# Sample rows of one output projection in fp32 on four column groups in the first sweep, their scores in three parts, the last rows in halves

## Chip, cores and metric

The kernel runs on one core of one Trainium2 chip. The metric is the device time of one execution in microseconds (us); lower is better. PE is TensorE, ACT ScalarE, DVE VectorE, POOL GpSimd and SP the engine that issues the DMAs.

## What is computed

Two layers of a streaming encoder, for 1024 prompt rows and for 32 sample rows of running streams (width 1024). The even layer ends with an output projection over the two branch outputs, the odd layer is causal attention with a forget bias:

```python
# even layer
o = jnp.einsum('ble,ed->bld', jnp.concatenate([ya, yb], axis=-1), w_out)   # 2048 x 1024 weights
x = x + rmsnorm(o, g_post)
# odd layer, for each of 8 heads
s = q @ k_all.T * scale + f_q - f_k          # prompt rows: 1024 keys; sample rows: 256 cached + 32 own
s = where(key_pos <= query_pos, s, -inf)
y = silu(z) * (softmax(s) @ v_all)
x = x + rmsnorm(y @ w_out_odd, g_post)
```

## The kernel before

**Precision.** Nearly all products are made from two parts. A value is split into a high part in fp32r and the rest in fp32r (`WH`/`WL` for weights, `HH`/`HL` and `YSH`/`YSL` for activations), and each product is three fp32r matmuls: high by high, low by high, high by low. Attention's scores, its probabilities times values, and the products with the state of the recurrence are true fp32 matmuls; the trace shows each of these as two records.

**Even output projection (`out_step`, L1034 on).** The weights have 16 blocks of 128 rows by 1024 columns. The 1024 prompt rows are eight tiles of 128 (t = 0 to 7), the 32 sample rows are tile 8 (`SMP`, also `NB`). Each tile has a pair of PSUM banks (`PAIRS`: t = 0, 4, 8 have banks 6 and 7; 1, 5 have 0 and 1; 2, 6 have 2 and 3; 3, 7 have 4 and 5). The work is done in three sweeps over all 16 weight blocks: tiles 0 to 2, tiles 3 to 5, tiles 6, 7 and `SMP`. A step of one weight block in one sweep is a unit (u = 0 to 47), and each sweep loads its 16 blocks again. In a unit a prompt tile takes six matmuls of 512 columns. The sample tile takes four: its high rows and its low rows stand side by side in the stationary operand, so two products per bank do. Units 46 and 47 come together: tile `SMP` first, then 6, then 7, each over both units.

**How a unit's weights get there.** `load_rows` on SP loads 512 KB to one of two raw buffers, `WRAW[:, idx % 2]`. It waits until the low parts of the unit two earlier are made (`w_low`, `oe_lo`), since these read the same raw buffer. ACT (`prepare`) splits off the high part of the activations (`token_high`) and of the weights (`split_rows`), POOL and DVE (`lows`) each make the low part of one half of the weights' columns. `WHS`/`WLS` and `YSH`/`YSL` have three slots; `prepare(u)` waits until unit u - 3 is done (`p_chunk`, three counts for a unit). PE waits in `units_ready(u)`. At u = 5 SP also issues four other loads of 512 KB. In the sweeps 1 and 2 the tiles of the sweep before are normalised between the units: ACT `squares`, DVE `gained`, `mean`, `residual`, `normed_x1`, PE `turn_h1` (transposes, before units k = 6, 7 and 13 of the sweep), ACT `h1_high`, DVE `h1_low`; SP stores rows at k = 6 and 15 and loads others at k = 11 and 12. Each engine works strictly in the order that is written out.

**Scores (`scores`, L1163 on).** In a turn of the loop over heads PE runs the scores, transposes and values of head t between the projections of head t + 1. The sample rows' scores are one fp32 matmul of 288 columns on 32 stationary columns, to partitions 0 to 31 of `PB[3]`. In the first seven heads DVE adds the mask of the last 32 keys and the forget bias and takes maxima; in the last head (`masked`) a bf16 matmul of the identity with `MASKD` adds the mask in PSUM.

**End.** The odd output projection ends with tile 7 in two halves of 512 columns. After each half ACT squares it, DVE multiplies it by the gain (`out_gained`), then `out_mean`, ACT's root and `out_rows` (one DVE instruction of 1024 columns), and SP stores 512 KB.

## Time and profile before

| | us |
|---|---|
| median of 3 runs | 1559.44 (1559.19 to 1560.11) |
| the profiled execution | 1558.85 |
| its span, first to last instruction | 1557.1 |
| PE busy, granted clock | 1526.9 (98%), 0.998 |
| first sweep of the even output projection | 65.3 |
| second sweep | 68.6 |
| third sweep, to the start of the last matmul of tile 7 | 61.6 |

The profiled execution's time is 1.75 us above its span. Start times count from the first instruction. A matmul's duration in a record is longer than its distance from the next one, since matmuls overlap in the array; distances between starts are what counts. An engine's "idle before" names who released it.

### The profile page before, as it was taken

The numbers are of one execution on the slowest core, as the hardware profiler recorded it, in microseconds if no ns is written. First come the engines' busy times: TensorE is split into PE (matmuls) and PEld (weight loads), VectorE is DVE, ScalarE is ACT, GpSimd is POOL, SyncE is SP. The second block draws the span as 40 slices with busy tenths as digits, with TensorE's granted clock in tenths as the row PEclk, the third lists the DMA queues.
The fourth block names the chain that finished last, engine by engine and source line by source line (L and its number), as shares of the span: only waits on it lengthen the run. The fifth ranks groups of instructions, "written<-read, shape, count | busy, mean of one in ns | idle before, by whom it ended". The sixth has DMA issues, their size and how long they took to land.

```text
span 1557.1 us, 26394 instructions
## 1 busy us (share of the span) xinstructions
PE 1526.9 (98%) x9409; PEld 1413.2 (91%) x9409; DVE 830.2 (53%) x1921; ACT 675.4 (43%) x1258; POOL 444.6 (29%) x268
## 2 busy tenths in 40 slices
PE   7999999999999999999999899999999999999998
PEld 6999999999999999988888898999999999988786
DVE  5547777776884231446475244545454554545532
ACT  6434443443233322345465344544454545455321
POOL 1214544452121111244343231322222222314200
PEclk9999999999999999999999999999999999999999
DMA  5122122213102111254456446624241424213122
GB/s 156 43 71 75 61 86 79 73 33 98 42 27 58 41 40 40 69 185 152 162 187 144 62 76 46 76 47 70 36 75 42 68 43 72 47 59 143 55 99 72
DMA packets 129513, 121.11 MB, mean 78 GB/s; under 512 B 10291, under 2 KB 113293, under 8 KB 129453
## 3 DMA queue, kind: packets, MB, share of 16 engines
q1 hardware_dynamic: 129452, 120.32, 31.7%
q8 instruction: 37, 0.61, 0.2%
q14 instruction: 24, 0.19, 0.0%
HBM read 101.64 MB, written 18.66 MB: 77 GB/s over the span
## 4 chain that ended last, share of the span: by engine, by line
PE 90%; ACT 4%; DVE 3%; issue 2%; DMA 0%; POOL 0%; SPq 0%; ACTq 0%; DVEq 0%; POOLq 0%
PE PB L767 85%; PE PB L771 5%; ACT L1358 1%; ACT L1826 1%; DVE SB L1955 0%; ACT SB L1920 0%; ACT WH L1352 0%; DVE XT L1958 0%; DVE M L1958 0%; ACT SQJ L1392 0%; DMA XS<-in_x_prompt_dram 0%; DMA WOR<-in_w_out_odd_dram 0%; DVE XS L1955 0%; DVE ST L1958 0%; POOL WL L633 0%
## 5 line engine op out<-in xcount | busy, mean ns | idle before, releaser
L767 PE MATMUL PB<-HH,WH 128*128 128x352 f32 x1872 | 626.5, 335 | 2.6 <-DVE HL L1951 1.6
L767 PE MATMUL PB<-HH,WL 128*128 128x352 f32 x1872 | 602.3, 322 | 0.0
L767 PE MATMUL PB<-HL,WH 128*128 128x352 f32 x1872 | 601.4, 321 | 0.0
L767 PEld LDWEIGHTS PB<-HH,WH 128*128 128x128 f32 x1872 | 351.9, 188 | 17.2 <-issue 9.2
L767 PEld LDWEIGHTS PB<-HL,WH 128*128 128x128 f32 x1872 | 352.9, 189 | 5.8 <-issue 3.3
L767 PEld LDWEIGHTS PB<-HH,WL 128*128 128x128 f32 x1872 | 352.1, 188 | 0.0
L633 POOL TENSOR_TENSOR WL<-WRAW,WH 128x1024 fp32r<-128x1024 f32 x81 | 199.3, 2460 | 525.6 <-ACT WH L1352 518.8
L1352 ACT ACTIVATE WH<-WRAW 128x1024 fp32r<-128x1024 f32 x112 | 118.0, 1053 | 14.4 <-DMA WRAW<-in_w_out_even_dram 6.3
L1920 ACT ACTIVATE SB<-SB,small 128x128 f32<-128x128 f32 (+8 forms) x72 | 53.9, 748 | 105.9 <-DVE small L1955 105.9
L767 PE MATMUL PB<-PT,VTOK 128*128 128x128 f32 (+2 forms) x624 | 81.5, 274 | 0.0
L767 PEld LDWEIGHTS PB<-PT,VTOK 128*128 128x128 f32 (+1 forms) x624 | 78.3, 191 | 1.5
L767 PE MATMUL PB<-KALL,QT 128*128 128x512 f32 (+4 forms) x208 | 78.0, 482 | 0.0
L1951 DVE TENSOR_TENSOR Y<-PB,Y 128x128 f32 (+3 forms) x72 | 20.2, 280 | 108.3 <-PE PB L767 108.2
L661 POOL TENSOR_TENSOR M<-M,CBT 128x512 f32<-128x512 f32 (+1 forms) x48 | 62.2, 1322 | 47.4 <-ACT M L1544 47.4
L767 PE MATMUL PB<-WH,YSH 128*128 128x512 f32 x192 | 75.1, 391 | 0.0
L767 PE MATMUL PB<-WL,YSH 128*128 128x512 f32 x192 | 74.8, 389 | 0.0
L685 POOL TENSOR_TENSOR WL<-WRAW,WH 128x512 fp32r<-128x512 f32 x30 | 53.5, 1785 | 65.5 <-ACT WH L1352 65.5
L1352 ACT ACTIVATE PT<-PB 128x512 f32<-128x512 f32 (+3 forms) x112 | 45.9, 447 | 55.4 <-PE PB L771 55.3
L1951 DVE TENSOR_TENSOR UG<-UG,ZG 128x1056 f32<-128x1056 f32 x8 | 12.2, 1529 | 105.5 <-ACT ZG L1372 105.5
L767 PE MATMUL PB<-WH,YSL 128*128 128x512 f32 x172 | 66.9, 389 | 0.0
L711 POOL TENSOR_TENSOR NRM<-QT 128x352 f32<-128x352 f32 x24 | 20.0, 833 | 145.8 <-ACT QT L1352 145.8
L1951 DVE TENSOR_TENSOR SB<-PB,MASKD 128x128 f32<-128x128 f32 (+1 forms) x63 | 17.6, 279 | 82.4 <-PE PB L767 82.4
(316 smaller groups left out, 2424.7 us busy)
## 6 DMA issues: line engine op xcount, KB each, us to landing
WRAW<-in_w_out_even_dram SPq DMA_DIRECT2D x48, 512.0 KB, 3.5
WRAW<-in_w_in_even_dram SPq DMA_DIRECT2D x44, 512.0 KB, 3.8
WRAW<-in_w_in_odd_dram SPq DMA_DIRECT2D x32, 512.0 KB, 8.2
ACSB<-acs_rows SPq DMA_DIRECT2D x16, 528.0 KB, 5.3
NFB<-nf_rows SPq DMA_DIRECT2D x8, 656.0 KB, 3.8
XS<-in_x_prompt_dram SPq DMA_DIRECT2D x8, 512.0 KB, 6.3
XT<-in_x_prompt_dram SPq DMA_DIRECT2D x8, 512.0 KB, 5.2
x_rows<-OG SPq DMA_DIRECT2D x8, 512.0 KB, 5.8
```

The costliest lines, as they stand in the source:

```text
L633: pool.tensor_tensor(WL[:, slot(w), :, :], WRAW[:, slot(w), :, :], WH[:, slot(w), :, :].bitcast(f32), ALU.subtract).then_inc(S("w_low"), 1)
L661: pool.tensor_tensor(m, m, CBT[0:rows, g, b0:b0 + nb, 0:rows], ALU.mult).then_inc(S("m"), 1)
L685: pool.tensor_tensor(WLS[SLOT3[u % 3]][:, HALF:D], raw[:, HALF:D], WHS[SLOT3[u % 3]][:, HALF:D].bitcast(f32), ALU.subtract).then_inc(S("w_ ...
L711: last = pool.tensor_tensor(NRM[:, n, cols], src, src, ALU.mult)
L767: return pe.matmul(out, lhsT, rhs, start=start, stop=stop)
L771: return pe.transpose(out, in_, IDENT[0:n, 0:n])
L1352: return act.activation(out, in_, ACT.Copy, scale=scale)
L1358: act.add_instruction(mybir.InstLoadActFuncSet(name=nc.get_next_instruction_name(), act_func_set_id=LN_EXP_SET, ins=[], outs=[]))
L1826: act.activation(Y1[:, p, :], Y1[:, p, :], ACT.Silu).then_inc(S("zs"), 1)
L1920: act.activation(SB[0:rows, 0:width], SB[0:rows, 0:width], ACT.Exp, scale=SCALE, bias=NBIAS[0:rows, :], accum_out=RSUM[0:rows, :]).then_in ...
L1951: return dve.tensor_tensor(out, a, b, op)
```

## The change

It has three parts. First, the sample rows leave the third sweep. In each unit of the first sweep PE makes four fp32 matmuls of 256 columns, which use the activations and the raw weights without splitting (`out_sample`); each writes to its own 32 partitions of `PB[4]`. They stand ahead of the unit's tiles, in unit 0 behind them. The load of a raw buffer now waits for them too (units 2 to 17). After unit 15's, ACT copies the sums to `SMPS` ahead of the squares, and tile 3 waits for the copy, as `PB[4]` is its bank. Second, in seven heads the sample rows' scores are three fp32 matmuls of 96 columns on three groups of partitions of `PB[3]`, followed by the mask as a bf16 matmul, and DVE takes three parts without a mask. Third, at the end `out_mean(8)` goes ahead of the last `out_gained`, and the last rows are made and stored in two halves.

```diff
+            if idx >= W_OE + 2 and idx < W_OE + 18:
+                sp.wait_ge(S("smp_mm"), idx - 1 - W_OE)
...
-            sp.wait_ge(S("y_done"), n + 1)
-            sp.dma_start(dst, X1T[n % 2][0:rows, :]).then_inc(S(f"y_stored{n % 2}"), 16)
+            parts = 2 if n == len(FINAL) - 1 else 1
+            for c in range(parts):
+                cols = slice(c * (D // parts), (c + 1) * (D // parts))
+                sp.wait_ge(S("y_done"), n + 1 + c)
+                sp.dma_start(dst[:, cols], X1T[n % 2][0:rows, cols]).then_inc(S(f"y_stored{n % 2}"), 16)
...
-                if t != SMP:
-                    mm(out, ysl[:, own], wh[:, cols], start=False, stop=False)
+                mm(out, ysl[:, own], wh[:, cols], start=False, stop=False)
...
+        def out_sample(u):
+
+            k = u % 16
+            pe.wait_ge(S(f"w_raw{u % 2}"), loads_of_slot(tile_no(W_OE + u, 1, 0)))
+            y = YB[:, k, SEQ:TOK] if k < 8 else YA[:, k - 8, SEQ:TOK]
+            raw = WRAW[:, (W_OE + u) % 2, :, :].rearrange("p k c -> p (k c)")
+            for q in range(4):
+                last = mm(sample_part(q), y, raw[:, q * PART:(q + 1) * PART], start=k == 0, stop=k == 15)
+            last.then_inc(S("smp_mm"), 1)
...
-            tiles = range(3 * sweep, 3 * sweep + 3)
+            tiles = range(3 * sweep, min(3 * sweep + 3, NB))
...
+                if 0 < u < 16:
+                    out_sample(u)
...
+                        if t == 3:
+                            pe.wait_ge(S("smp_out"), 1)
...
-                    out_step(t, u, j).then_inc(S("p_chunk"), 1)
+                    out_step(t, u, j).then_inc(S("p_chunk"), 2 if t == NB - 1 else 1)
+                if u == 0:
+                    out_sample(u)
...
-        for j, t in ((2, SMP), (0, 6), (1, 7)):
+        for j, t in ((0, 6), (1, 7)):
             out_step(t, 46, j)
-            out_step(t, 47, j).then_inc(S("p_chunk"), 2)
+            out_step(t, 47, j).then_inc(S("p_chunk"), 3)
...
+            if b == NB and not masked:
+                for k in range(3):
+                    cols = slice(SEQ + k * PART3, SEQ + (k + 1) * PART3)
+                    mm(sample_scores(k), q, KALL[:, cols], stop=k < 2)
+                mm(sample_scores(2)[:, PART3 - DEC:PART3], IDENTB[0:rows, 0:rows], MASKD[0:rows, 0:rows],
+                   start=False).then_inc(S("sc_mm"), 1)
+                return
...
-            return copy(high[:, 0:2 * P + DEC], src[:, 6 * P:TOK])
+            return copy(high[:, 0:2 * P], src[:, 6 * P:SEQ])
...
-                    copy(OGT[2][0:DEC, c * HALF:(c + 1) * HALF], bank[DEC:2 * DEC, :]).then_inc(S("o_sq"), 1)
+                    act.wait_ge(S("p_chunk"), 3 * (W_OE + 46))
+                    copy(OGT[2][0:DEC, c * PART:(c + 1) * PART], SMPS[c * DEC:(c + 1) * DEC, :]).then_inc(S("o_sq"), 1)
                 else:
...
+            if u == 15:
+                act.wait_ge(S("smp_mm"), 16)
+                copy(SMPS[:, :], PB[4][:, 0:PART]).then_inc(S("smp_out"), 1)
...
             else:
-                tt(YSL[u % 3][:, 0:2 * P], src[:, 6 * P:SEQ], high[:, 0:2 * P].bitcast(f32), ALU.subtract)
-                last = tt(high[:, 2 * P + DEC:2 * P + 2 * DEC], src[:, SEQ:TOK], high[:, 2 * P:2 * P + DEC].bitcast(f32),
-                          ALU.subtract)
+                last = tt(YSL[u % 3][:, 0:2 * P], src[:, 6 * P:SEQ], high[:, 0:2 * P].bitcast(f32), ALU.subtract)
...
-                dve.wait_ge(S("o_sq"), 2 * place(t) + c + 1)
+                dve.wait_ge(S("o_sq"), 2 * place(t) + (2 if t == SMP else c + 1))
...
-                    tt(og[0:DEC, cols], bank[0:DEC, :], og[0:DEC, cols], ALU.add).then_inc(S("o_g"), 1)
+                    q = 2 + c
+                    dve.tensor_copy(og[0:DEC, q * PART:(q + 1) * PART], SMPS[q * DEC:(q + 1) * DEC, :]).then_inc(S("o_g"), 1)
...
-                    own = width if not project else width - rows
-                    n = (own + 511) // 512
+                    parts = project and i == NB
+                    own = width - rows if project and not parts else width
+                    step = PART3 if parts else 512
+                    n = (own + step - 1) // step
...
-                    if project:
+                    if own == width:
+                        order(dve.memset(MX[0:rows, n:n + 1], -3.0e38))
+                    else:
...
-                        c0, c1 = k * 512, min(own, k * 512 + 512)
-                        order(dve.tensor_tensor_reduce(SB[0:rows, c0:c1], PB[3 + k][0:rows, 0:c1 - c0],
-                                                       NFB[0:rows, key0 + c0:key0 + c1], 1.0, -3.0e38,
+                        c0, c1 = k * step, min(own, (k + 1) * step)
+                        part = slice(k * DEC, (k + 1) * DEC) if parts else slice(0, rows)
+                        scored = sample_scores(k) if parts else PB[3 + k][0:rows, 0:c1 - c0]
+                        order(dve.tensor_tensor_reduce(SB[0:rows, c0:c1], scored,
+                                                       NFB[part, key0 + c0:key0 + c1], 1.0, -3.0e38,
                                                        ALU.add, ALU.max, MX[0:rows, k:k + 1]))
...
-        def out_rows(n):
+        def out_rows(n, parts=1):
...
-            stt(X1T[n % 2][0:rows, :], FOG[n % 2][0:rows, :], ORR[0:rows, n:n + 1], X1T[n % 2][0:rows, :],
-                ALU.mult, ALU.add).then_inc(S("y_done"), 1)
+            for c in range(parts):
+                cols = slice(c * (D // parts), (c + 1) * (D // parts))
+                stt(X1T[n % 2][0:rows, cols], FOG[n % 2][0:rows, cols], ORR[0:rows, n:n + 1], X1T[n % 2][0:rows, cols],
+                    ALU.mult, ALU.add).then_inc(S("y_done"), 1)
...
-        for h in range(6, 18):
+        for h in range(6, 17):
             out_gained(h)
             if h % 2 == 1:
                 out_mean(h // 2)
                 out_rows(h // 2)
+        out_mean(8)
+        out_gained(17)
+        out_rows(8, parts=2)
```

## Rows read from the trace of the kernel before

**Rows 1.** Page, first part: busy time, share of the span, instructions.
```profile
PE 1526.9 (98%) x9409; PEld 1413.2 (91%) x9409; DVE 830.2 (53%) x1921; ACT 675.4 (43%) x1258; POOL 444.6 (29%) x268
```

**Rows 2.** Busy time by stretch: engines with instructions, PEclk, DMA share, GB/s.
```profile
649.97:715.30 65.33, 65.33 (x290) 54.06 (x290) 31.01 (x40) 26.89 (x40) 30.21 (x17) 1.00 0.48 161
```

**Rows 3.** The chain that ended last, in order of time: start us, us, what.
```profile
745.75 20.46 PE PB L767 x90
...
811.25 18.19 PE PB L767 x80
...
831.51 2.33 DVE XT L1958
```

**Rows 4.** Timeline of PE: start us, us, operation, count [idle before, releaser].
```profile
133.51 1.06 PE L767 MATMUL PB<-CT,ST 128*128 128x128 f32 x8
134.50 1.09 PE L767 MATMUL PB<-M,XD 128*64 128x128 f32 x16
135.52 0.43 PE L767 MATMUL PB<-HH,WH 128*128 128x352 f32 x1
```

**Rows 5.** The same timeline, asked for the stretch 134.45 to 134.52 only.
```profile
134.50 0.33 PE L767 MATMUL PB<-M,XD 128*64 128x128 f32 x2
```

**Rows 6.** Timeline of PE: scores of the sample rows in one head.
```profile
970.90 1.04 PE L771 MATMUL PB<-IDENT,SB 128*128 128x128 f32 x8
971.87 0.67 PE L767 MATMUL PB<-KALL,QT 128*32 128x288 f32 x2
972.47 0.43 PE L767 MATMUL PB<-HH,WH 128*128 128x352 f32 x1
972.73 0.32 PE L767 MATMUL PB<-HL,WH 128*128 128x352 f32 x1
```

**Rows 7.** Timeline of PE: scores of the sample rows in the last head.
```profile
1483.36 0.67 PE L767 MATMUL PB<-KALL,QT 128*32 128x288 f32 x2
1483.96 0.18 PE L767 MATMUL PB<-MASKD,IDENTB 32*32 32x32 bf16 x1
1484.07 0.50 PE L767 MATMUL PB<-WH,YH 128*128 128x512 f32 x1
```

**Rows 8.** Timelines of SP, ACT and POOL: one load and its two splits.
```profile
673.00 2.49 SPq L483 DMA_DIRECT2D WRAW<-in_w_out_even_dram  x2
...
676.42 1.06 ACT L1352 ACTIVATE WHC<-WRAW 128x1024 fp32r<-128x1024 f32 x1 [1.24 <-DMA WRAW<-in_w_out_even_dram]
...
677.56 1.80 POOL L685 TENSOR_TENSOR WLC<-WRAW,WHC 128x512 fp32r<-128x512 f32 x1 [3.02 <-ACT WHC L1352]
...
679.38 0.33 SPq L483 DMA_DIRECT2D WRAW<-in_w_out_even_dram  x1
```

**Rows 9.** Timelines of SP and ACT: the load after four others.
```profile
664.46 0.33 SPq L483 DMA_DIRECT2D WRAW<-in_w_out_even_dram  x1
...
670.03 1.06 ACT L1352 ACTIVATE WH<-WRAW 128x1024 fp32r<-128x1024 f32 x1 [3.01 <-DMA WRAW<-in_w_out_even_dram]
```

**Rows 10.** Timelines of ACT and DVE at the end of the first sweep.
```profile
712.76 0.58 ACT L1665 ACTIVATE JUNK<-PB 128x512 f32<-128x512 f32 x1
...
713.53 1.40 DVE L1951 TENSOR_TENSOR OG<-PB,POSTB 128x512 f32<-128x512 f32 x2
```

**Rows 11.** Timelines of POOL, SP, ACT and PE in the third sweep.
```profile
781.52 1.80 POOL L685 TENSOR_TENSOR WL<-WRAW,WH 128x512 fp32r<-128x512 f32 x1 [2.28 <-ACT WH L1352]
...
798.31 0.33 SPq L483 DMA_DIRECT2D WRAW<-in_w_out_even_dram  x1
...
803.10 1.06 ACT L1352 ACTIVATE WH<-WRAW 128x1024 fp32r<-128x1024 f32 x1 [0.39 <-DMA WRAW<-in_w_out_even_dram]
...
833.88 1.09 PE L771 MATMUL PB<-IDENT,XT 128*128 128x128 f32 x8 [0.83 <-DVE XT L1958]
```

**Rows 12.** Timelines of DVE at the end of the kernel, and DMA.
```profile
1551.36 0.69 DVE L1951 TENSOR_TENSOR FOG<-PB,POSTF 128x512 f32<-128x512 f32 x1 [4.87 <-ACT JUNKF L1787]
...
1552.68 1.28 DVE L1958 SCALAR_TENSOR_TENSOR X1T<-FOG,small,X1T 128x1024 f32<-128x1024 f32 x1 [0.50 <-ACT small L1603]
...
out_dram<-X1T SPq DMA_DIRECT2D x1, 512.0 KB, 2.6
```

**Rows 13.** Timeline of DVE after the third sweep.
```profile
855.79 1.28 DVE L1958 SCALAR_TENSOR_TENSOR OG<-OG,small,XT 128x1024 f32<-128x1024 f32 x1 [1.11 <-DMA XT<-in_x_prompt_dram]
```

## What I expect and why

> **What bounds the kernel.** I read the page's busy times first: PE is at work for 98% of the span [rows 1]. That alone doesn't say that PE is the bound in each stage, so next came the busy times by stretch: in the first sweep of the even output projection PE is busy for all of its 65.33 us, ACT and POOL for less than half of it [rows 2]. The chain of waits in order of time says the same of the later sweeps: long pieces of nothing but matmuls, 90 in 20.46 us and 80 in 18.19 us, so 0.2273 us for one of 512 columns, with a short break for a DVE result once in a while [rows 3]. There the reader is to see two things: a matmul removed is worth 0.2273 us as long as PE stays the bound, and a unit takes PE 18 x 0.2273 = 4.09 us in the first two sweeps and 16 x 0.2273 = 3.64 us in the third. Whether PE stays the bound depends on the feeding of the weights, which I read in the timelines of SP, ACT and POOL [rows 8].
>
> **Matmuls removed.** Tile SMP had 4 matmuls in each of 16 units: 64 x 0.2273 = -14.5 us, all of it PE time in the third sweep. A unit there takes PE 12 x 0.2273 = 2.73 us.
>
> **The sample step added.** Each of 16 units of the first sweep gets four fp32 matmuls of 256 columns with 32 stationary columns. Their price rests on whether the four run side by side. The trace has a case with two column groups: 16 records of 64 stationary columns take 1.02 us, from 134.50 to 135.52, while 8 records of 128 stationary columns over as many moving columns take 0.99 [rows 4]. So two halves cost what one whole costs. The narrow look shows the first two started within 0.02 us [rows 5]. I take four groups to do what two do. One fp32 matmul of 288 columns on 32 stationary ones, in the same mode, takes 0.60 us to the next matmul's start [rows 6]; 256 columns take at most a ninth less, so 0.55. There is more at both ends. The records on 128 stationary columns follow each other by about 0.11 us; 8 of them from 133.51 would end at 134.41, and the next kind starts at 134.50: 0.09 to go in [rows 4]. And the first matmul afterwards is followed only after 0.26 us (972.47 to 972.73) where 352 columns otherwise take 0.16: 0.10 to come out [rows 6]. In all 0.55 + 0.09 + 0.10 = 0.74, with some 0.02 for three more starts 0.76 us. 16 x 0.76 = +12.2 us. The bounds: 0.55 if the ends are hidden (8.8 us), and 4 x 0.5 + 0.2 if nothing overlaps (35 us). I take 0.76, since rows 4 and 6 show both ends paid.
>
> The Trainium skill gives 2.38 times for three column tiles (TensorE: Matmul & The Clock Gate, Measured speedup vs the span model), thus less than three; an estimate from that would put some 0.1 us more on each step, and 2 us on the sum.
>
> **Waits in the first sweep.** A raw buffer is now free only when PE has read it. A load takes 3.42 us until ACT splits it (673.00 to 676.42), ACT's split is 1.14 us ahead of POOL's, POOL's takes 1.80, and SP reacts at 679.38: 6.38 us for one turn of a buffer [rows 8]. Before, it could begin as soon as the low part was made; now it begins about 0.65 us into unit u - 2, where PE's sample step ends. For most units that is hidden: two units are 2 x 4.85 = 9.7 us, and 0.65 + 6.4 = 7.0. It isn't hidden in unit 2, since unit 0's sample step stands at its end: 4.8 + 6.35 = 11.1 us against 9.7, a wait of 1.4. Unit 6 has its load behind four others, where a load took 5.57 us (664.46 to 670.03) [rows 9]: 2.2 us more, which eats the slack of 2.7 nearly up; I add 0.3 for queueing. Together +1.7 us, between 0 and 4.
>
> **The border of the first two sweeps.** On ACT `prepare(17)` stands ahead of the copy to `SMPS` and of four squares. Its load now starts 0.65 us into unit 15 and its split ends at 0.65 + 3.4 + 1.1 = 5.15, the copy at 5.5; unit 16 would start at 4.85, and its first tile waits for the copy: 0.7. The squares, then DVE's products by the gain (0.77 behind, 712.76 to 713.53, 1.40 for two [rows 10]), hold the banks of tiles 4 and 5: the second tile could start at 5.5 + 1.6 + 0.8 = 7.9 but is due at 6.9. I count 0.9 for tiles 4 and 5. Together +1.6 us, between 0 and 3. Queued behind the copy on ACT are the squares and `prepare(18)`, which has a unit to spare.
>
> **The third sweep stops being bound by PE.** Here is the main step. Two units now take PE 5.46 us, but a raw buffer's turn is 6.38, and there are two buffers: a unit per 3.19 us at best. The low part of unit 33 is made at 781.52 + 1.80 = 783.32 [rows 11], 0.6 us ahead of unit 32 (783.9). 14 turns later, unit 47's is ready at -0.6 + 14 x 3.19 = 44.1 us after the sweep's start; units 46 and 47 then take 24 x 0.2273 = 5.5. That makes 49.6 against 61.8 before: a gain of 12.2, not 14.5. Five transfers of rows share the queue in this sweep; with two of them a load took 4.79 us until its split (798.31 to 803.10), 1.4 more [rows 11]. Some 2.2 us of that fall on the last turns, which have no slack. Last, PE transposes tile 5 ahead of unit 45 and before waited 0.83 us for DVE there [rows 11]; DVE makes its 2.33 us instruction [rows 3] only behind its low part of unit 46. That part is made at about 42 us, so the transposes come at 44.2, unit 45 at 45.1 and the end at 45.1 + 2.7 + 5.5 = 53.3 us. The gain is 8.5; waits +6.1, between 2.3 and 9. I carried these waits through all 48 units; done the same way for the kernel before, with its own waits, this gives 0.3 us less than recorded.
>
> **Behind the sweep.** The rows that tile 7 is added to are loaded late, and DVE waits for them until 855.79 [rows 13]. Their load stands behind POOL's split that starts when tile 6 is done, as far from the end of tile 7 as before. So the sample rows' earlier sums gain nothing here: 0, and up to +1 for the load before it that comes closer.
>
> **Scores in seven heads.** Before: 0.60 us to the next matmul [rows 6]. After: two passes of 96 columns in three groups, 0.60 x 96 / 288 = 0.20, but with the fixed part that doesn't shrink some 0.28; then the mask, 0.11 us to the next matmul [rows 7]. 0.39 against 0.60: 7 x -0.2 = -1.4 us, between -1.5 and +1.5 (groups one after the other). DVE has one part more and a mask less; PE doesn't wait for it there.
>
> **The end.** `out_mean(8)` goes ahead of 0.69 us of DVE work, so the root is ready by the time this ends, and the last rows start 0.4 us earlier; a second instruction takes some 0.1 of that back. The second store holds half the bytes of one that took 2.6 us to land [rows 12]: 0.6 us less. -1.0 us, between -1.4 and 0.
>
> **Sum.** -14.5 + 12.2 + 1.7 + 1.6 + 6.1 - 1.4 - 1.0 = +4.7 us on the profiled 1558.85: 1563.5. The median of the runs stands 0.6 above that execution: 1564.1 us. 0.2% of the time, about what a measurement of this kernel can tell from no change, is 3.1 us.
>
> **Rivals.** *The feeding keeps up* (0.15). If the turn of a buffer takes under 5.46 us, or the units stored ahead last the sweep, the 9.4 us of waits vanish: 1554.7, faster. For it: POOL and ACT are idle for half the time [rows 2]. Against it: the turn is a chain, not a load, and rows 8 have 6.38. *Half of the waits* (0.12), as when loads land sooner while alone: 1559.4, no change. *The groups overlap by their order only* (0.08). Each fp32 matmul is two passes on its own group; if starts keep program order, the second pass of one overlaps the first of the next, five passes in a row, not two. That adds 3 x 0.21 us per unit, 10 us, of which waits give back 1: about 1573.4. Against it: the first two records of different groups start together [rows 5], where by this order the second record would have been the same group's. The Trainium skill has that rule: matmuls keep program order in start and in end (TensorE: Matmul & The Clock Gate, The mechanism); no row here speaks for it. *No overlap of four groups at all* (0.05): about 1583.
>
> **How the numbers follow.** The forecast has 0.60, with its own range of 1560 to 1568.5. With the first two rivals the range 1554 to 1568.5 holds 0.8. Faster by over 0.2%: 0.15. Within: 0.12 and the lower fifth of the forecast, 0.24. Slower: 0.61.
>
> **What will show it.** In the timeline of PE of after, in the first sweep: a unit every 4.85 us, and four fp32 starts within 0.02 us of each other; 4 passes or 8 one after the other would be a rival. In the third sweep: units 3.2 us apart from about u = 40, PE waiting for POOL's `WL` or ACT's split for a DMA, and a wait of some 4 us for DVE's XT ahead of the last transposes. If units stay at 2.73 us there, my main step is wrong. At u = 2 a wait of 1.4 us, and one for the copy at unit 16. The sample rows' scores: 0.2 us less per head. If the whole is faster than 1559, look at the third sweep first.

## Result and the profile after

The kernel with the change takes 1576.4 us (median, 1575.98 to 1577.12) against 1559.8 us before (1559.19 to 1561.85): ratio 1.0105, 95% interval 1.0087 to 1.0122. It is slower, as forecast, but by 16.6 us where 4.7 were forecast, and outside the range. The profiled execution took 1575.98 us with a span of 1574.2.

First the page of after, busy times, and then the busy time of each engine in the three sweeps (columns as in [rows 2]):

```profile
PE 1531.7 (97%) x9508; PEld 1407.9 (89%) x9508; DVE 836.9 (53%) x1904; ACT 674.8 (43%) x1259; POOL 444.3 (28%) x268
...
650.01:737.73 87.72, 81.50 (x420) 57.75 (x418) 36.10 (x37) 25.28 (x35) 29.54 (x17) 0.96 0.38 125
737.73:807.46 69.73, 68.83 (x313) 56.39 (x314) 43.05 (x61) 37.10 (x74) 29.80 (x17) 1.00 0.51 167
807.46:863.50 56.04, 48.90 (x217) 39.19 (x216) 38.09 (x53) 33.74 (x67) 27.13 (x15) 0.97 0.62 182
```

The reader is to see PE busy for 81.5 of 87.7 us in the first sweep, where before it was busy without a break [rows 2], and a granted clock under 1.00 in the first and the third sweep. With each sweep counted from its first matmul to the first of the next, the kernel before needs 65.4, 68.7 and 61.9 us. So the sweeps give 22.3 + 1.1 - 5.9 = +17.5 us. From the end of the third sweep to the first matmul of the attention stage's norm (`NRMH`) it is 58.1 against 55.9 us, +2.2; from there to the start of the kernel's last matmul, which holds the heads, -1.9; behind that matmul 6.1 against 6.9, -0.9. With 0.2 us ahead of the sweeps that is +17.1, as much as the spans differ by.

The waits of PE over the three sweeps of after (what it waited for, by whom: us in total, times, longest):

```profile
PE PB L785 <- DMA WRAW<-in_w_out_even_dram: 5.6, 2, 3.7
PE PB L789 <- DVE XT L2003: 4.5, 2, 4.0
PE PB L789 <- DVE HL L1996: 1.9, 1, 1.9
PE PB L789 <- ACT JUNK L1707: 1.3, 1, 1.3
PE PB L785 <- ACT SMPS L1392: 0.7, 1, 0.7
```

The first line is new: PE itself waits for a DMA of weights, in two places. PE's timeline shows the first of them, in unit 1:

```profile
653.99 0.39 PE L785 MATMUL PB<-WL,YSH 128*128 128x512 f32 x1
654.31 0.64 PE L785 MATMUL PB<-WRAW,YB 128*32 128x256 f32 x8
658.66 0.64 PE L785 MATMUL PB<-WRAW,YB 128*32 128x256 f32 x8 [3.71 <-DMA WRAW<-in_w_out_even_dram]
659.23 0.78 PE L785 MATMUL PB<-WH,YSH 128*128 128x512 f32 x1
659.80 0.63 PE L785 MATMUL PB<-WH,YSL 128*128 128x512 f32 x1
660.23 0.63 PE L785 MATMUL PB<-WL,YSH 128*128 128x512 f32 x1
```

ACT had begun to split unit 1's weights at 648.64, ten us earlier. Its own load can't be what it waits for. The wait in the code is on `w_raw{u % 2}`, but unit u's load has the index `W_OE + u`, and `W_OE` is 45: the count is that of the other buffer. So every odd unit waits until the load of unit u + 1 has landed. That load is issued only when unit 0's sample step is over (655.06) and lands at about 658.5. In unit 5 the same wait meets the load that stands behind four others, for 1.85 us. The even units wait for unit u - 1's load, which is there.

The last three lines show the second thing. Starts are 0.43 us apart (659.80 to 660.23), not 0.23: the matmul of 512 columns runs at half the clock. Windows of after within the four such stretches that lie between 18 us and the last matmul:

```profile
659.80:662.40 2.60, 2.60 (x8) 2.01 (x7) 2.07 (x2) 0.21 (x1) 1.66 (x1) 0.50 0.60 202
683.84:686.40 2.56, 2.56 (x7) 2.00 (x6) 1.09 (x1) 0.53 (x1) 0.67 (x1) 0.50 0.50 189
853.85:857.20 3.35, 3.35 (x9) 2.65 (x8) 1.89 (x3) 1.25 (x3) 1.79 (x1) 0.50 0.10 8
901.80:905.20 3.40, 3.40 (x14) 3.40 (x13) 0.00 (x0) 0.00 (x0) 0.00 (x0) 0.52 0.60 59
```

Granted clock 0.50: the lower of its two levels, 1.2 and not 2.4 GHz. Each stretch is 3.4 us long with its edges and does half the work, so it costs some 1.7 us. Before each of them PE had stood idle: 3.7, 1.9, 4.0 and 1.6 us. The profile of before has none between 18 us and its last matmul. The other three executions of after have mean clocks of 0.993 to 0.995 too, so the stretches are not peculiar to this one.

In the third sweep the last turns (the transposes of tile 5) wait as forecast (columns as above; compare 0.83 us in [rows 11]):

```profile
848.27 0.39 PE L785 MATMUL PB<-WLC,YSHD 128*128 128x512 f32 x1
852.69 1.09 PE L789 MATMUL PB<-IDENT,XT 128*128 128x128 f32 x8 [4.03 <-DVE XT L2003]
853.54 0.52 PE L785 MATMUL PB<-WH,YSH 128*128 128x512 f32 x1
853.85 0.63 PE L785 MATMUL PB<-WH,YSL 128*128 128x512 f32 x1
```

The sample step itself, in the narrow look at its first 0.03 us and then in unit 3:

```profile
654.31 0.42 PE L785 MATMUL PB<-WRAW,YB 128*32 128x256 f32 x4
...
670.03 0.64 PE L785 MATMUL PB<-WRAW,YB 128*32 128x256 f32 x8
670.60 0.50 PE L785 MATMUL PB<-WH,YSH 128*128 128x512 f32 x1
```

Four matmuls on four column groups start within 0.02 us. Unit 4's step begins at 674.91, so a unit takes 4.88 us; 4.85 were forecast. The Trainium skill says that matmuls are in program order in start and in end (TensorE: Matmul & The Clock Gate, The mechanism). The four matmuls taken whole don't contradict it. Their two passes taken singly do: were they kept in order, matmul by matmul, four starts could not lie within 0.02 us (654.307 to 654.327) with the four second passes 0.24 us behind. There the measurement decides, and it was on the passes that the prediction's rival stood.

Scores of the sample rows in one head, and the end of the kernel (answering to [rows 6] and [rows 12]):

```profile
991.78 0.37 PE L785 MATMUL PB<-KALL,QT 128*32 128x96 f32 x6
992.08 0.18 PE L785 MATMUL PB<-MASKD,IDENTB 32*32 32x32 bf16 x1
992.20 0.43 PE L785 MATMUL PB<-HH,WH 128*128 128x352 f32 x1
...
1569.34 0.21 DVE L1999 TENSOR_SCALAR small<-small 128x1 f32<-128x1 f32 x1 [4.87 <-ACT JUNKF L1832]
1569.47 0.68 DVE L1996 TENSOR_TENSOR FOG<-PB,POSTF 128x512 f32<-128x512 f32 x1
1570.25 1.41 DVE L2003 SCALAR_TENSOR_TENSOR X1T<-FOG,small,X1T 128x512 f32<-128x512 f32 x2
```

0.42 us from the first score to the next work, against 0.60: a head is 72.5 us long where it was 72.7 (from the first transposes of one to those of the next).

### The profile page after: what moved, and what is told of

Same layout as the page of the kernel before. It is cut to its first block and busy times, and to the rows that moved or that the text cites. A ratio compares the mean times of both kernels' runs of the same rounds, so it can differ in the third digit from the quotient of the medians.

```text
span 1574.2 us, 26570 instructions
## 1 busy us (share of the span) xinstructions
PE 1531.7 (97%) x9508; PEld 1407.9 (89%) x9508; DVE 836.9 (53%) x1904; ACT 674.8 (43%) x1259; POOL 444.3 (28%) x268
## 5 line engine op out<-in xcount | busy, mean ns | idle before, releaser
L785 PE MATMUL PB<-PT,VTOK 128*128 128x128 f32 (+2 forms) x624 | 81.5, 274 | 0.0
L785 PE MATMUL PB<-WH,YSH 128*128 128x512 f32 x172 | 70.1, 408 | 1.1 <-ACT SMPS L1392 0.7
L1996 DVE TENSOR_TENSOR UG<-UG,ZG 128x1056 f32<-128x1056 f32 x8 | 12.2, 1528 | 105.6 <-ACT ZG L1412 105.6
L785 PE MATMUL PB<-WL,YSH 128*128 128x512 f32 x172 | 68.3, 397 | 0.0
L1996 DVE TENSOR_TENSOR NRML<-NRM,NRMH 128x352 fp32r<-128x352 f32 x48 | 44.1, 919 | 21.9 <-ACT NRMH L1392 21.2
```

Of the source, the lines that this page charges most:

```text
L785: return pe.matmul(out, lhsT, rhs, start=start, stop=stop)
L1996: return dve.tensor_tensor(out, a, b, op)
```

## Experiments

The sweeps' lengths from all traces (us, from first matmul to first matmul; the third up to the next stage) carry most of what follows:

| kernel | first | second | third | half clock from (us; 650 to 910) |
|---|---|---|---|---|
| before | 65.4 | 68.7 | 61.9 | none |
| after | 87.7 | 69.7 | 56.0 | 659, 683, 854, 902 |
| mended index | 80.6 | 69.7 | 58.8 | 826, 846 (6.8 us long), 897 |
| one sample step | 70.4 | 68.7 | 56.3 | 834 |
| three raw buffers | 77.9 | 68.7 | 52.9 | 839, 887 |
| early norm | 81.1 | 69.7 | 56.4 | 851 |
| three buffers, early norm | 77.9 | 68.7 | 49.1 | none |
| filled idle | 82.4 | 69.7 | 54.9 | 662, 894 |

### The index mended

```diff
-            pe.wait_ge(S(f"w_raw{u % 2}"), loads_of_slot(tile_no(W_OE + u, 1, 0)))
+            pe.wait_ge(S(f"w_raw{(W_OE + u) % 2}"), loads_of_slot(tile_no(W_OE + u, 1, 0)))
```

> The changed kernel with one index mended: TensorE's sample step of unit u waits for the count of its own weight buffer, (45 + u) % 2, and no longer for the other buffer's. Theory W (the wrong wait is the cause of the two stalls of 3.7 and 1.9 us in the first sweep, and each stall of the half clock behind it, 1.7 us each): both stalls and both stretches at the half clock go, the first sweep falls from 86.9 to some 79 to 80 us, the whole from 1576.4 to about 1569 (1568 to 1571). Rival F (the loads themselves are late, the wait only shows it: unit 6 waits for load 6 anyway): TensorE stops at the next unit instead, at least the stall of 1.9 us stays with its clock, and the time is 1572 to 1576. The third sweep stays at 56 us in both.

1571.66 us; 1.0071 of before (1.0055 to 1.0086). Both waits for a DMA are gone, and so are both stretches at half clock in the first sweep, which is 7.1 us shorter. But 4.7 us came out, not the 7.4 expected, and the time is outside the 1568 to 1571 given. The third sweep, which was to stay at 56 us, is 2.7 us longer: the clock fell there twice instead of once, the second time for 6.8 us, and its last wait is 0.5 longer. The last turns, and the windows of the two stretches (the second from its first matmul on):

```profile
848.25 0.69 PE L789 MATMUL PB<-IDENT,XT 128*128 128x128 f32 x2 [4.56 <-DVE XT L2003]
...
825.60:829.00 3.40, 3.40 (x11) 2.66 (x10) 1.89 (x3) 2.03 (x3) 1.78 (x1) 0.51 0.47 154
...
848.25:852.85 4.60, 4.60 (x15) 4.02 (x16) 2.35 (x4) 2.04 (x3) 1.79 (x1) 0.50 0.26 30
```

And one honest wait has come to light, in unit 2:

```profile
654.84 1.07 PE L785 MATMUL PB<-WRAW,YB 128*32 128x256 f32 x16
655.85 0.50 PE L785 MATMUL PB<-WH,YSH 128*128 128x512 f32 x1
...
662.12 0.64 PE L785 MATMUL PB<-WRAW,YB 128*32 128x256 f32 x8 [1.86 <-POOL WLC L691]
```

This is the wait that the prediction had at 1.4 us: unit 2's load is held by unit 0's sample step. (The first line is the steps of units 0 and 1, which stand side by side.) Theory W holds for the waits; rival F fell, unit 6 does not wait.

### The second and third part alone

The kernel before, with the diff's parts for scores and end only.

> The kernel before with the second and third part of the change alone: the sample scores in three parts in seven heads, and the end in halves. The sweeps stay as before. If both give what the prediction said (1.4 and 1.0 us): 2.4 us under the kernel before, about 1557.4. Rival: the scores' gain is taken by another wait in the heads, and only the end shows: 1558.8.

1558.20 us against 1560.43; 0.9988 of before (0.9979 to 0.9997). Together they give 2.2 us, about what was forecast; in the trace the stretch with the heads is 1.7 us shorter and the end 0.8, and the sweeps are those of before. The trace also has half clock from 883 us, which the trace of before has not, so its span is only 0.8 us shorter. This kernel is faster than both, if only just by its interval. So the first part alone costs 1576.4 - 1558.2 = some 18 us.

### Only one sample step

The sample rows' products of the other fifteen weight blocks are left out. The index is mended here as well, and ACT's copy to `SMPS` waits for one step.

```diff
-                if 0 < u < 16:
-                    out_sample(u)
...
-            if idx >= W_OE + 2 and idx < W_OE + 18:
+            if idx == W_OE + 2:
                 sp.wait_ge(S("smp_mm"), idx - 1 - W_OE)
```

> The changed kernel with the sample step in unit 0 alone; the other fifteen products of the sample rows in the even output projection are left out, and so is the wait of the loads for them. Theory (all that the first sweep lost is the sample step and what hangs on it): the first sweep comes back to 66 us, second and third sweep stay at 70.4 and 56.0, with the idle before the last turns (4.4 us) and the half clock behind it; 1576.4 - 86.9 + 66.1 = 1555.6. Rival (the late feeding of the third sweep comes from the order that the first sweep leaves behind): the third sweep changes by more than 1 us. Rival (the three sweeps share one limit, the loads): the first sweep does not come back to 66 but stops at the turn of the load.

1559.49 us; 0.9992 of before (0.9982 to 1.0001). The third sweep is 56.3 us, within 0.3 of after's, so its waits don't come from the first. The first sweep came back to 70.4 only: the load of unit 2 still waits for unit 0's step.

```profile
PE PB L785 <- POOL WLC L691: 2.7, 1, 2.7
PE PB L785 <- POOL WL L691: 0.8, 1, 0.8
```

This sweep is 4.3 us over the 66.1 expected: those two waits and the step that was left in. The expectation had counted this hold at nothing, although the prediction had priced it. The wait is 0.8 us longer than with the index mended alone, about the step of unit 1 that no longer stands before it. The median is 3.9 us above what was expected. The profiled execution took 1556.45 us, the fastest of ten, so the two figures are not of the same execution.

### A third raw buffer

```diff
+    RAWS = (WRAW[:, 0, :, :], WRAW[:, 1, :, :], HX[:, :, 7 * P:8 * P])
...
+                sp.wait_ge(S("w_low"), idx - 2)
+                sp.wait_ge(S("oe_lo"), u - 2)
+                if u < 19:
+                    sp.wait_ge(S("smp_mm"), u - 2)
+                sp.wait_ge(S(f"w_raw{idx % 2}"), loads_of_slot(tile_no(idx, 1, 0)) - 16)
+            sp.dma_start(RAWS[SLOT3[u % 3]], src.rearrange("p (k c) -> p k c", c=P)).then_inc(S(f"w_raw{idx % 2}"), 16)
```

> The mended index of the first run and a third buffer for the raw weight rows, so that the load of unit u waits for the split of unit u - 3 instead of u - 2. Theory B (the third sweep waits for a turn of load, split and release over two buffers, 3.2 us for a unit against 2.73 us of TensorE's work): the gaps of 1.6, 2.3 and 4.4 us in the third sweep and the half clock behind the last (1.7) go, the sweep takes 46 to 48 us, the whole 1560 to 1562. Rival A (ScalarE's and VectorE's own order of work sets the turn): the sweep stays within 2 us of 56, the whole 1567 to 1570. Rival H (the transfers themselves are too slow for two in flight): the loads take longer from issue to landing than now, and the sweep gains under half.

1561.49 us; 1.0005 of before (0.9996 to 1.0014). That is 10.2 us less than with the index alone. The busy times of its first and third sweep:

```profile
649.78:727.66 77.88, 77.88 (x420) 55.59 (x418) 27.09 (x41) 27.30 (x41) 31.04 (x17) 1.00 0.45 148
...
796.34:849.21 52.87, 48.52 (x217) 39.26 (x216) 38.70 (x53) 33.34 (x67) 26.25 (x15) 0.97 0.63 182
```

In the first sweep PE is busy for all of it: here the sample step is measured clean. 77.88 - 65.41 = 12.47 us for 16 steps, 0.78 us each; 0.76 was forecast. In the third sweep the wait ahead of the last turns is 3.0 us where it was 4.6, with the half clock behind it. The sweep is 52.9 us, not the 46 to 48 that theory B expected. The whole came out where it put it only because the first two sweeps gave 3.8 us as well (no wait in unit 2 and at the border). The wait of the middle turns (1.9 us) went; something else holds the last ones as well.

### The norm of tile 5 one unit earlier

```diff
-                if k == 10:
+                if k == (9 if sweep == 2 else 10):
                     residual(t0 + 2)
-                if k == 11:
+                if k == (10 if sweep == 2 else 11):
                     mean_x1(t0 + 2)
-                if k == 12:
+                if k == (11 if sweep == 2 else 12):
                     normed_x1(t0 + 2)
```

and the same on ACT for its square. Once with two raw buffers, once with three.

> The mended index with two raw buffers, and in the third sweep alone the last tile's residual, square and norm are each issued one unit earlier on VectorE and ScalarE (units 9, 10 and 11 instead of 10, 11 and 12). Theory S (the written order makes the idle of 5.0 us before the last turns: on VectorE the norm stands behind the low parts of unit 46, which wait for TensorE to leave unit 43): that idle falls under 2 us, and the half clock behind it (1.7 us) goes; about 1567 against 1571.7. Rival B (the two raw buffers are the limit, the norm is late only because all feeding is): the same idle shows ahead of the units instead, and the time stays within 1.5 us of 1571.7.

> The third raw buffer and the earlier norm together. If the order of the norm is what is left of the third sweep's idle (3.4 us before the last turns, and 1.7 us of half clock), the sweep falls from 52.9 to some 48 us and the whole from 1561.5 to about 1556.5. If the loads or ScalarE's own work set the pace, the idle comes back ahead of unit 45 or 46 and the time is over 1559.

With two buffers: 1567.97 us, 1.0048 of before (1.0031 to 1.0065). With three: 1561.80, 1.0003 (0.9994 to 1.0013), and a profiled span of 1555.3. With two buffers the wait ahead of the turns falls from 4.6 to 1.4 us, but a new one of 2.6 us for POOL's low part stands one unit behind it, and the sweep is 56.4 us long:

```profile
PE PB L785 <- POOL WLC L691: 2.6, 1, 2.6
PE PB L789 <- DVE XT L2003: 1.9, 2, 1.4
```

What this trace gained is mostly the clock (one fall where there were three), and hardly the waits: its third sweep has 7.3 us of them, the one with the index alone 7.7. Both expectations came true in part: the time is near theory S's 1567, and the idle did come back ahead of a unit, as rival B had it. With three buffers the sweep is 49.1 us, and of its waits only the one ahead of tile 3's turns (1.3 us, put down to ACT's squares in the other traces) is over 0.8. So **two limits lie over each other** at the end of the third sweep. Of the 4.6 us ahead of the last turns, 3.0 stay when the buffers' turn is taken away; when the order is taken away, 1.4 stay and 2.6 come back one unit later. Only both together bring the sweep near PE's own 47.2 us. The earlier norm is worth 0.4 us of waits with two buffers and 3.0 with three. The third buffer is the larger step by itself: the sweep falls by 5.9 us, some 2.3 of them clock.

The median doesn't show the last step: 1561.49 us with three buffers, 1561.80 with the norm as well. A later section is on that.

### The idle filled

```diff
+            if b == 5:
+                pe.wait_ge(S("h1_lo"), 10)
+                for n in range(16):
+                    mm(PB[0][:, :], HH[:, n % KT, 0:P], HH[:, n % KT, 0:4 * P], start=True, stop=True)
             pe.wait_ge(S("xn1"), place(b) + 1)
```

> The mended index, and in the idle before the last turns of the third sweep (4.95 us) sixteen matmuls of 512 columns on columns that are there already, 3.6 us of work; their result is written over. Theory C (the half clock behind the idle comes from the idle): no stretch at the half clock behind these turns, 1.7 us gained: about 1570 against 1571.7. Rival D (the half clock has another cause, a limit on power over the sweep): the clock falls all the same, or falls earlier, and the time is 1571.7 or more.

1569.90 us; 1.0056 of before (1.0040 to 1.0073), 1.8 us less than with the index alone, where 1.7 were expected (the two intervals overlap). PE around the last turns:

```profile
843.13 3.83 PE L785 MATMUL PB<-HH 128*128 128x512 f32 x16
847.50 0.77 PE L789 MATMUL PB<-IDENT,XT 128*128 128x128 f32 x5 [0.54 <-DVE XT L2007]
```

With work in the idle, the clock stays at 1.00 behind the turns, in the same place where it had been 0.5 in after and in the run with the mended index. That is one execution. What gives it weight is the count over all sixteen traces (18 us to the last matmul): all ten idles of PE of 3.0 to 4.6 us had a fall of the clock, between 2.2 us before their end and 1.2 us behind it. Filled, this one had none. So theory C, that PE's idleness costs the half clock, is well supported; rival D's limit over the sweep is not what these traces show. In the first sweep of this execution the clock did fall, at 662 us behind an idle of 1.9 us, where the run with the mended index kept it behind the same idle. Whether a short idle brings the clock down thus varies between executions.

### Why three buffers and the early norm give 1562 and not 1557

Ten executions lay at 1557.1, 1558.3, and eight between 1561.1 and 1563.1. So the kernel was profiled again.

> The kernel with the third raw buffer and the earlier norm a second time, for its trace: its first profile had no stretch at the half clock behind 18 us and a span of 1555.3 us, while eight of its ten executions lay between 1559.4 and 1561.3. Theory C (the executions differ by where the clock falls, with the same waits): this profile has the same waits within 0.3 us each, and one to three stretches at the half clock, each about 1.7 us, that make up the difference of the spans. Rival: the waits themselves differ, by a transfer that comes later.

1562.16 us, span 1560.4. The three sweeps agree with the first profile within 0.1 us. Theory C asked for the same waits everywhere, and that failed; the rival is right: behind the sweep PE idles for 3.7 us in place of 1.0. Timelines of ACT, DVE and POOL, first of the 1557 us execution, then of the 1562 us one:

```profile
840.71 1.06 ACT L1412 ACTIVATE WH<-WRAW 128x1024 fp32r<-128x1024 f32 x1 [2.15 <-DMA WRAW<-in_w_in_odd_dram]
...
842.55 0.59 DVE L2351 COPY OG<-SMPS 32x256 f32<-32x256 f32 x2 [1.58 <-ACT OG L1412]
...
843.07 2.40 POOL L659 TENSOR_TENSOR WL<-WRAW,WH 128x1024 fp32r<-128x1024 f32 x1 [3.85 <-PE PB L805]
```

```profile
841.85 1.06 ACT L1412 ACTIVATE WH<-WRAW 128x1024 fp32r<-128x1024 f32 x1 [4.02 <-DMA WRAW<-in_w_in_odd_dram]
...
843.68 2.24 DVE L2351 COPY OG<-SMPS 32x256 f32<-32x256 f32 x2 [2.68 <-ACT OG L1412]
...
843.07 2.40 POOL L659 TENSOR_TENSOR WL<-WRAW,WH 128x1024 fp32r<-128x1024 f32 x1 [4.76 <-PE PB L805]
...
857.14 0.66 PE L805 MATMUL PB<-HH,WH 128*128 128x352 f32 x1 [3.70 <-POOL WL L659]
```

A load of weights is split 1.14 us later. ACT's copies of sample rows, and so DVE's (both new with the change), come later with it. DVE's now begin inside POOL's split (843.07 to 845.47): the first takes 1.93 us and ends 0.14 us behind the split, the second 0.28, together 2.24 in place of 0.59. Delay and hold are 2.8 us, and the next splits and PE's wait are later by about that. Here the clock falls, from 856.5 us and for 6.8 us, which it didn't in the other execution. The spans differ by 5.1 us; 2.8 us are this, and the half clock is enough for the rest. Two runs then took DVE's copies away from this place, first with an operation of two inputs:

```diff
-                    dve.tensor_copy(og[0:DEC, q * PART:(q + 1) * PART], SMPS[q * DEC:(q + 1) * DEC, :]).then_inc(S("o_g"), 1)
+                    tt(og[0:DEC, q * PART:(q + 1) * PART], SMPS[q * DEC:(q + 1) * DEC, :],
+                       SMPS[q * DEC:(q + 1) * DEC, :], ALU.max).then_inc(S("o_g"), 1)
```

> The kernel with the third raw buffer and the earlier norm; VectorE's two copies of sample rows behind the sweeps are made as a maximum of the rows with themselves, an operation with two inputs. In two executions of that kernel the two copies took 0.59 us, where they began 0.5 us before GpSimd's split of the weights (2.40 us), and 2.24 us, where they began 0.6 us behind it and ended when it ended; the wait of TensorE at 853 us was 1.3 and 4.0 us. Theory G (a copy on VectorE waits until GpSimd's running operation is over, an operation with two inputs does not): the two take under 1.2 us also where they begin inside GpSimd's split; the wait falls to 2.4 us or less in every execution; median 1561.8 - 1.6 = about 1560.2, and less if the half clock behind the wait goes too. Rival M (the memory behind both is the limit, whatever the operation): they still end with GpSimd's split, and the time stays at 1561.8.

1562.59 us; 1.0009 of before (0.9998 to 1.0020). A miss: the pair took 2.52 us and PE waited 3.9. What rival M expected is what came:

```profile
843.63 2.52 DVE L2021 TENSOR_TENSOR OG<-SMPS 32x256 f32<-32x256 f32 x2 [2.69 <-ACT OG L1412]
```

Then with all four copies on ACT:

```diff
-                    copy(OGT[2][0:DEC, c * PART:(c + 1) * PART], SMPS[c * DEC:(c + 1) * DEC, :]).then_inc(S("o_sq"), 1)
+                    for q, done in ((2 * c, "o_sq"), (2 * c + 1, "o_g")):
+                        copy(OGT[2][0:DEC, q * PART:(q + 1) * PART], SMPS[q * DEC:(q + 1) * DEC, :]).then_inc(S(done), 1)
```

> The kernel with the third raw buffer and the earlier norm; ScalarE makes all four copies of the sample rows behind the sweeps (0.42 us apart), and VectorE none. Theory G2 (any operation of VectorE that works from and to the memory it shares with GpSimd waits for GpSimd's running split; as a maximum of two inputs the two took 2.52 us and ended with it): the square of the sample rows comes about 1.4 us earlier where the load of these weights lands late, TensorE's wait of 3.7 to 3.9 us behind the sweep falls to about 2.4, and the median from 1561.8 to about 1560.4, lower where the half clock behind the wait goes too. Rival: another operation of the chain is held in its place and the wait stays over 3.5 us; the time stays at 1561.8.

1560.36 us; 1.0000 of before (0.9991 to 1.0010), 1.4 us less, as expected, though the intervals of the two kernels overlap. The four copies took 1.72 us while POOL's split ran beside them, and PE's wait fell from 3.7 to 2.3 us, with the load as late as in the 1562 us execution:

```profile
842.97 1.72 ACT L1412 ACTIVATE OG<-SMPS 32x256 f32<-32x256 f32 x4
```

So DVE's copies were the cause of this piece of the wait. Nor can the memory itself be the limit, as rival M had it, since ACT copied the same rows beside the split. The clock fell at 857 us all the same. Why the load of these weights lands early in some executions was not found.

### Sample steps in pairs

Three runs on top of three buffers and the early norm: the steps of two units made together in the odd unit; the four loads behind unit 5 spread as well; and on top of that, in two separate runs, a split of weights ahead of two squares, and the copies on ACT with the copy to `SMPS` put ahead of unit 17's splits.

```diff
-                if 0 < u < 16:
+                if u < 16 and k % 2:
+                    out_sample(u - 1)
                     out_sample(u)
```

> As the run with both, and TensorE makes the sample step for two units at once, in every odd unit: eight changes to fp32 and back instead of sixteen. Theory P (of the 0.76 us of a step some 0.32 us are the changes into and out of the column groups): eight times 0.32 less, 2.6 us: about 1554. In the trace of the mended index two steps that stood side by side took 0.70 us from first to last start against 0.26 us for one, so 0.44 us for the second. Rival: the longer hold of the raw rows delays the loads and the gain goes in waits in the first sweep: no change, 1556.5.

> As the run with the sample steps in pairs, and the four transfers that stand behind the load of unit 5 (two rows spread over the partitions, two tiles of x) go one by one behind the loads of units 5, 7, 9 and 11. Theory L (the idle of 2.45 us ahead of unit 6 in the run with pairs comes from these four, since the load of unit 6 now waits longer for its buffer and then shares the engines with them): the idle and its half clock go, 1564.6 - 4.1 = about 1560.5. Rival (the longer hold of the raw rows alone makes it): the idle stays at unit 6 or comes at the next even unit, 1563 to 1565.

> As the run with the spread transfers, and ScalarE splits the weights of the stage behind the sweeps ahead of the squares of tile 7 instead of behind them. If the wait of 3.7 us for the low part of these weights comes from ScalarE's order, it falls by the 1.3 us of the squares, and the whole by 1.3 us against the run with spread transfers; if it comes from a late load it stays.

> The kernel with sample steps in pairs and spread transfers; the four copies on ScalarE, and ScalarE's copy of the finished sample rows at the border of the sweeps ahead of its splits for unit 17. If the pairs' gain of 2.6 us was lost at these two places (1.3 us of wait for the copy at the border, and 1.4 us behind the sweeps): 1562.5 - 2.7 = about 1559.8. If only the second place holds: 1561.1.

In pairs: 1564.59 us, 1.0021 (1.0010 to 1.0032), 2.8 slower than the run that it stands on. Raw rows are held longer, unit 6 waits 2.1 us for POOL and the border 1.5 us for the copy to `SMPS`: the rival. With the loads spread, 1562.54, 1.0005 (0.9992 to 1.0018): the wait at unit 6 is gone, the border's is 1.3; 2.0 of the 4.1 us expected came. With the split ahead of the squares, 1563.82, 1.0011 (0.9997 to 1.0025), 1.3 us more where 1.3 less were expected: the wait of 3.7 us for POOL's low part is gone, and one of 4.4 us for ACT's read into `FRAW` stands in its place. With the copies at their new places, 1561.61, 1.0001 (0.9991 to 1.0010), 0.9 us less where 2.7 were expected: the border now waits 1.8 us for the squares, which stand behind the copy and the splits. Pairs do save PE time: with the loads spread PE is busy for 144.5 us of the first two sweeps, against 146.1 without pairs. But the two sweeps together last 146.7 us, as before (146.6), since the saving went in waits at the border.

## Why the prediction missed

By its own terms, for the profiled execution:

- **Matmuls removed** (-14.5) and **sample step** (+12.2): right. The step measured 0.78 us against 0.76 (12.5 us in all), all four groups side by side. Both rivals about overlap fell.
- **Waits in the first sweep** (+1.7, between 0 and 4) and **border** (+1.6): this is the step that failed first and by most. The two sweeps became 23.4 us longer; less 12.5 for the steps, 10.9 us are waits. With the index mended it is 3.8, close to the 3.3 forecast. The other 7.1 us are the wait on the wrong buffer's count and the two falls of the clock behind it. The prediction read the wait as one for unit u's own load and never put numbers to it: `W_OE` is odd, so `u % 2` and `(W_OE + u) % 2` never agree. It named the units 2 and 6 as those at risk, and after has its waits one unit earlier, in 1 and 5.
- **Third sweep** (+6.1 of waits, 53.3 us long): its main step, that each unit takes half a buffer's turn, failed by its own sign. The units were to come 3.2 us apart, and "if units stay at 2.73 us there, my main step is wrong": 72 matmuls stand in a row from 832.05 to 848.27, 2.7 us a unit. PE waits instead ahead of the turns (1.3, 1.9 and 4.0 us), of which the prediction had the last, and there its some 4 us are right. The two buffers are a limit all the same, since a third took 3.4 us of these waits away (7.7 to 4.3, index mended). The waits come to 7.1 us where 6.1 were forecast, and 1.7 us of half clock come on top: the sweep took 56.0. That its length came near the forecast is in part luck.
- **Behind the sweep** (0): +2.2 us, of which 1.7 are a fall of the clock behind an idle that the kernel before has too, at full clock. The other 0.5 were not traced.
- **Scores** (-1.4) and **end** (-1.0): -1.9 and -0.9. Right, the first a little short.

Summed, the miss is 7.9 us in the first two sweeps (23.4 against 15.5), 2.5 in the third (-5.9 against -8.4), 2.2 behind it and 0.2 ahead of the sweeps, less 0.3 for scores and end: 12.5 us, as the executions show (1575.98 against 1563.5). Of these, some 6.8 us are four stretches at half clock, a term that the prediction did not have: it priced idle at its length.

The first part had little to win, since 12.5 us of sample steps stand against 14.5 us of matmuls. The best median of its mended versions is level with the kernel before (1560.36 against 1560.42), with waits of 2.3 and 1.3 us and one stretch at half clock left in its trace. That version holds the second and third part too, and these alone gave 1558.20: no median here shows a gain from the first part. Single executions do lie lower, down to 1556.9 us.

## What to carry over

Work out every index of an added wait in numbers for two units before pricing it: a wait on the wrong buffer is harmless in half of its uses and costs a load's turn in the rest. A new idle on PE is to be priced at its length and, with a chance, a stretch at half clock near it; a forecast with five new waits needs that term. Where a stage is made shorter for PE, look for all limits at the new pace, for a second limit can hide behind the first: the earlier norm took 0.4 us of waits off while the buffers' turn stood, and 3.0 us without it.

## What the hardware showed

- **The clock.** Between 18 us and the last matmul the sixteen traces have 26 stretches at 0.50 of PE's clock, 24 of them 3.4 us long, where about 1.7 us were lost each, and two 6.8 us long. Each came with an idle of 1.6 to 4.6 us: with all ten idles of 3.0 us or more, and with eight of the fifteen of 1.8 to 2.7. The idle for DVE's `INC` (at about 900 us in after; 1.6 us in 14 traces, 1.7 and 2.3 in the others) was followed by half clock in 9 of 16. Filled with work, an idle of 4.6 us was not. Executions of one kernel go with it: of 27 of the kernel before, those at a mean clock of 0.999 have spans of 1557.4 to 1559.3 us, those at 0.995 or 0.996 1560.8 to 1562.0.
- **VectorE and GpSimd.** Two operations of 32x256 from and to the on-chip memory took 0.59 us when they began before GpSimd's split. Where they began inside it, the first ended only when the split had (2.24 us for both as copies, 2.52 with two inputs). On ScalarE they ran beside it. The Trainium skill has this as an exclusive lock on a port pair that these two share, for VectorE's fast copies and for operations with two inputs from that memory (SBUF — State Buffer, SBUF: two separate sides); the traces agree, and by that rule the maximum of two inputs could not have helped.
- **Four column groups.** Four fp32 matmuls with 32 stationary and 256 moving columns take 0.78 us of PE's time, both changes of mode within it; a second such step right behind adds 0.44 us (0.70 against 0.26 us from first to last start).
